# Second attention of a two-layer kernel: blocks from last to first, the causal mask subtracted by VectorE, products a step later

## The reference, cut to what matters

```python
def _forgetting_attention(q, k, v, log_f):
    scale = ATT_HEAD_DIM ** -0.5
    fcum = jnp.cumsum(log_f, axis=-1)
    for blk in range(seqlen // ATT_BLOCK):          # 8 blocks of 128 queries
        q0, q1 = blk * ATT_BLOCK, (blk + 1) * ATT_BLOCK
        s = jnp.einsum('bhqd,bhkd->bhqk', q[:, :, q0:q1], k[:, :, :q1]) * scale
        s = s + fcum[:, :, q0:q1, None] - fcum[:, :, None, :q1]
        s = jnp.where(kpos[None, :] <= qpos[:, None], s, -jnp.inf)
        prob = jax.nn.softmax(s, axis=-1)
        outs.append(jnp.einsum('bhqk,bhkd->bhqd', prob, v[:, :, :q1]))
```

## Time and profile before

| | |
|---|---|
| time, median of 3 runs | 2603.03 us (2601.33 to 2605.16) |
| the profiled execution: its time, its span | 2604.71 us, 2602.9 us |
| TensorE busy, share of the span | 2530.3 us, 97% |
| VectorE, ScalarE, GpSimd busy | 1580.3, 1225.1, 1134.3 us |
| granted TensorE clock, mean | 0.991 |
| second attention | from about 1838 to 2330 us |

### The profile page before, as it was taken

The page is one execution under the profiler, slowest core; times in us unless marked ns, Lnnn a source line. Parts: engine busy times, 40 slices in busy tenths (PEclk is TensorE's granted clock), DMA queues, the critical chain, the costliest instruction groups (busy, mean ns, idle before and its releaser), DMA issues.

```text
span 2602.9 us, 32821 instructions
## 1 busy us (share of the span) xinstructions
PE 2530.3 (97%) x12946; PEld 2120.4 (81%) x12946; DVE 1580.3 (61%) x2413; ACT 1225.1 (47%) x1858; POOL 1134.3 (44%) x759
## 2 busy tenths in 40 slices
PE   5999999999999999999999999999999999999998
PEld 3788898877888888878788888888888888888886
DVE  7554899487555556665833367665666666654333
ACT  4243888344444443342543435543666666642132
POOL 0222444439787863444487234333322222235233
PEclk8999999999999999999999999999999999999998
DMA  6133001322222226553232322222111111167452
GB/s 272 65 121 130 1 1 66 114 79 92 89 81 78 92 102 242 179 174 122 90 117 102 122 73 90 90 84 71 65 49 49 49 59 60 54 213 273 148 184 97
DMA packets 84457, 275.81 MB, mean 106 GB/s; under 512 B 9392, under 2 KB 9520, under 8 KB 84304
## 3 DMA queue, kind: packets, MB, share of 16 engines
q1 hardware_dynamic: 84304, 273.71, 30.0%
HBM read 219.54 MB, written 54.13 MB: 105 GB/s over the span
## 4 chain that ended last, share of the span: by engine, by line
PE 81%; DVE 9%; ACT 5%; DMA 2%; issue 1%; POOL 1%; SPq 0%; DVEq 0%; ACTq 0%; POOLq 0%
PE ps L614 12%; PE ps L616 12%; PE ps L615 12%; PE ps L991 7%; PE ps L992 7%; PE ps L993 7%; PE ps L857 5%; PE ps L834 4%; PE ps L810 2%; PE ps L811 2%; PE ps L1048 2%; DVE wf L3056 2%; PE ps L1049 2%; PE ps L1050 2%; DVE wf L3081 1%
## 5 line engine op out<-in xcount | busy, mean ns | idle before, releaser
L3383 POOL TENSOR_TENSOR hl<-raw,hl 128x1024 fp32r<-128x1024 f32 x161 | 403.9, 2511 | 933.9 <-ACT hl L1407 933.5
L614 PE MATMUL ps<-ht,hl 128*128 128x512 f32 x1552 | 633.4, 408 | 15.0 <-DVE ht L2456 9.9
L616 PE MATMUL ps<-ht,hl 128*128 128x512 f32 x1552 | 608.3, 392 | 0.0
L615 PE MATMUL ps<-ht,hl 128*128 128x512 f32 x1552 | 607.8, 392 | 0.0
L614 PEld LDWEIGHTS ps<-ht,hl 128*128 128x128 f32 x1552 | 293.5, 189 | 75.4 <-DVE ht L2456 9.9
L616 PEld LDWEIGHTS ps<-ht,hl 128*128 128x128 f32 x1552 | 292.8, 189 | 64.1
L615 PEld LDWEIGHTS ps<-ht,hl 128*128 128x128 f32 x1552 | 294.0, 189 | 53.8 <-issue 1.5
L3459 POOL TENSOR_SCALAR wf<-wf,st 128x1024 f32<-128x1024 f32 (+2 forms) x192 | 168.8, 879 | 318.7 <-DVE st L2589 318.7
L1407 ACT ACTIVATE hl<-raw 128x1024 fp32r<-128x1024 f32 x163 | 171.3, 1053 | 178.9 <-PE ps L1050 66.6
L2396 DVE TENSOR_TENSOR ps<-ps,wf 128x512 f32<-128x512 f32 x116 | 80.8, 697 | 152.3 <-PE ps L993 152.1
L834 PE MATMUL ps<-cst,wf 128*128 128x128 f32 x1088 | 151.4, 274 | 3.8 <-POOL wf L3459 3.8
(11 more groups left out here) (287 smaller groups left out, 5314.8 us busy)
## 6 DMA issues: line engine op xcount, KB each, us to landing
raw<-in_wst SPq DMA_DIRECT2D x243, 512.0 KB, 3.6
wf<-scratch_rows SPq DMA_DIRECT2D x32, 512.0 KB, 5.0
scratch_g<-wf SPq DMA_DIRECT2D x22, 512.0 KB, 2.6
wf<-scratch_g SPq DMA_DIRECT2D x44, 256.0 KB, 4.2
wf<-in_xT SPq DMA_DIRECT2D x16, 512.0 KB, 7.7
htf<-in_wst SPq DMA_DIRECT2D x16, 512.0 KB, 15.4
scratch_ys<-wr SPq DMA_DIRECT2D x16, 512.0 KB, 4.5
ht<-scratch_ys SPq DMA_DIRECT2D x32, 256.0 KB, 5.9
```

The costliest lines, as they stand in the source:

```text
L614: self.op.matmul(out, wh, xh[:, c], start=(j == 0), stop=False)
L615: self.op.matmul(out, wh, xl[:, c], start=False, stop=False)
L616: t = self.op.matmul(out, wl, xh[:, c], start=False, stop=(j == kt - 1))
L3383: self.op.tensor_tensor(K.hl[:, u * 2048 + 1024:u * 2048 + 2048], K.raw[:, i % 3 * 1024:(i % 3 + 1) * 1024], hi.bitcast(F32), ALU.subtract ...
```

## The change

It has five parts, all in the second attention.

1. Every head's query blocks go from 7 to 0: a block in step `s` has `8 - s % 8` key blocks where it had `s % 8 + 1`. A pair of blocks for `back` now begins with the longer one, so `back` takes its length from the odd block number.
2. The mask matmul L815 is gone. VectorE has a new method `mask`: one subtraction of 128 x 128 from the forget-gate row in SBUF, once for each block, ahead of the `top` that reads it.
3. `back` for a pair stands at odd steps, right behind the scores and ahead of the fillers, on blocks `s - 3` and `s - 2`; it stood at even steps behind the transposes, on blocks `s - 2` and `s - 1`. ScalarE and VectorE copy its product out ahead of their part of `turn`.
4. On VectorE the reciprocal `soft(s + 1)` stands behind `top(s + 2)` and `mask(s + 3)`, where it was `soft(s + 2)` at the end of step `s`; the transposes' low part is last in the step. ScalarE's and GpSimd's orders stay, but for the place of `back`.
5. `fills` has another table. The number of fillers in a pair stays: 24 in steps -2 to 13 (27 for the last pair).

```diff
@@ fills
-    if s < 2:
-        return (0, 3 if p == 7 else 2, 3, 3)[s + 2]
     if p == 7 and s > LAST_FILL:
         return {13: 1, 14: 4, 16: 3}.get(s, 0) if own else 0
     if p == 7:
-        return (2, 1, 2, 1, 2, 2, 2, 1, 2, 1, 2)[s - 2]
-    return 2 if s in (4, 6, 10, 12) else int(s < 14)
+        return (0, 3, 4, 1, 3, 1, 3, 1, 2, 1, 3, 1, 2, 1, 1)[s + 2]
+    return (0, 3, 4, 1, 3, 1, 2, 0, 2, 0, 3, 1, 2, 0, 2, 0)[s + 2] if s < 14 else 0
@@ TensorEngine.scores
-            t = self.op.matmul(out, qs, K.wrr(kl)[:, c], start=False, stop=not diag)
-            if diag:
-                self.consts()
-                self.wait_ge(*K.at("maskr"))
-                t = self.op.matmul(K.ps[pair][:, nk - 128:nk], K.idr[:, :], K.maskr[:, :],
-                                   start=False, stop=True)
+            t = self.op.matmul(out, qs, K.wrr(kl)[:, c], start=False, stop=True)
@@ TensorEngine.back
-        nk = qt + 1 if causal else 8
+        nk = (qt | 1) + 1 if causal else 8
...
-            c0 = 128 if causal and j == qt else 0
+            c0 = 128 if causal and j == nk - 1 else 0
@@ TensorEngine.attend2
                 if s + 2 < 16:
                     sc(s + 2)
+                if s >= 3 and s % 2 == 1:
+                    g = 16 * p + s - 2
+                    hi, lo, _ = pt2(K, (g // 2) % 2)
+                    self.back(2, g, 7 - (s - 2) % 8, hi, lo, 6 + (s - 2) // 8, True,
+                              (("vstack2", p),))
                 self.fill(fills(p, s, True))
...
                 if 0 <= s < 16:
-                    self.turn(2, 16 * p + s, s % 8, 9 + (16 * p + s) % 3, True)
-                if s >= 2 and s % 2 == 0:
-                    g = 16 * p + s - 1
-                    hi, lo, _ = pt2(K, (g // 2) % 2)
-                    self.back(2, g, (s - 1) % 8, hi, lo, 6 + (s - 1) // 8, True,
-                              (("vstack2", p),))
+                    self.turn(2, 16 * p + s, 7 - s % 8, 9 + (16 * p + s) % 3, True)
@@ VectorEngine
+    def mask(self, h, qt):
+
+        K = self.K
+        c = K.w(20 + h % 2)[:, qt * 128:qt * 128 + 128]
+        self.wait_ge(*K.at("fcum", h))
+        self.wait_ge(*K.at("maskr"))
+        self.op.tensor_tensor(c, c, K.maskr[:, :].bitcast(F32),
+                              ALU.subtract).then_inc(*self.done("masked", h, qt))
@@ VectorEngine.attend2
                 if s + 2 < 16:
-                    self.top(2, g + 2, 2 * p + (s + 2) // 8, (s + 2) % 8, 9 + (g + 2) % 3, True)
+                    if s == -2:
+                        self.mask(2 * p, 7)
+                    self.top(2, g + 2, 2 * p + (s + 2) // 8, 7 - (s + 2) % 8, 9 + (g + 2) % 3, True)
+                    if s + 3 < 16:
+                        self.mask(2 * p + (s + 3) // 8, 7 - (s + 3) % 8)
...
+                if 0 <= s + 1 < 16:
+                    self.soft(2, g + 1)
+                if s >= 3 and s % 2 == 1:
+                    self.back(2, g - 2, (s - 2) // 8, 7 - (s - 2) % 8, w(22))
                 if 0 <= s < 16:
-                    self.turn(2, g, s % 8, pt2(K, (g // 2) % 2), True)
-                if s + 2 < 16:
-                    self.soft(2, g + 2)
-                if s >= 2 and s % 2 == 0:
-                    self.back(2, g - 1, (s - 1) // 8, (s - 1) % 8, w(22))
+                    self.turn(2, g, 7 - s % 8, pt2(K, (g // 2) % 2), True)
```

More of the change, by code:

```diff
@@ L805, in scores @@
             out = K.ps[pair][:, c]
-            diag = causal and c.stop == nk
             self.bank_free(2 * pair + half)
@@ L841, in back @@
         K = self.K
-        nk = qt + 1 if causal else 8
+        nk = (qt | 1) + 1 if causal else 8
         for gg in (g - 1, g):
-            for half in range((((qt if gg == g else qt - 1) + 1 if causal else 8) + 3) // 4):
+            for half in range(((qt + g - gg + 1 if causal else 8) + 3) // 4):
                 self.wait_ge(*K.at("plo", A, gg, half))
@@ L1286, in sc @@
                 k = 2 + 2 * h
-                self.scores(2, 16 * p + s, 2 * p + h, s % 8, h, k, k + 1, True,
+                self.scores(2, 16 * p + s, 2 * p + h, 7 - s % 8, h, k, k + 1, True,
                             (("stacklo", "q2", p, h), ("stacklo", "k", p, h),
@@ L2206, in attend2 @@
                 g = 16 * p + s
+                if s >= 3 and s % 2 == 1:
+                    if s == 3 and p:
+                        self.wait_ge(*K.at("stored_ya", p - 1))
+                    self.back(2, g - 2, (s - 2) // 8, 7 - (s - 2) % 8, w(22))
                 self.fill(fills(p, s))
@@ L2213, in attend2 @@
                 if 0 <= s < 16:
-                    self.turn(2, g, s % 8, pt2(K, (g // 2) % 2)[0], True)
+                    self.turn(2, g, 7 - s % 8, pt2(K, (g // 2) % 2)[0], True)
                 if s + 2 < 16:
-                    self.soft(2, g + 2, (s + 2) % 8, 9 + (g + 2) % 3, True)
-                if s >= 2 and s % 2 == 0:
-                    if s == 2 and p:
-                        self.wait_ge(*K.at("stored_ya", p - 1))
-                    self.back(2, g - 1, (s - 1) // 8, (s - 1) % 8, w(22))
+                    self.soft(2, g + 2, 7 - (s + 2) % 8, 9 + (g + 2) % 3, True)
                 if s == 15 and p < 7:
@@ L2575, in top @@
             if g >= 3:
-                self.wait_ge(*K.at("turn", A, g - 3, ((g - 3) % 8) // 4))
-            self.wait_ge(*K.at("fcum", h))
+                self.wait_ge(*K.at("turn", A, g - 3, (7 - (g - 3) % 8) // 4))
+            self.wait_ge(*K.at("masked", h, qt))
             self.op.tensor_tensor_reduce(pw, ps, K.w(20 + h % 2)[:, 0:nk], 1.0, -3.0e38,
@@ L3674, in attend2 @@
                 if s + 2 < 16:
-                    self.weigh(2, g + 2, (s + 2) % 8, 9 + (g + 2) % 3, True)
+                    self.weigh(2, g + 2, 7 - (s + 2) % 8, 9 + (g + 2) % 3, True)
                 if p == 7 and s == LAST_FILL:
```

## The result

The changed kernel takes 2626.94 us in the median (2624.21 to 2628.03), beside 2604.1 us for the kernel before, measured with it: a ratio of 1.0087, with a 95% interval of 1.0075 to 1.0100. It is 23 us slower, where 2587 us and at most 2597 were forecast. The profiled execution has a span of 2626.2 us.

The account below looks back on a forecast made before the run. The prediction took TensorE's queue of matmuls, busy 59.79 of 60 us, as the bound. Its terms -13.3 - 2.9 + 0.5 = -15.7 us took 2604.71 to 2589.0, a median of 2587 us expected, range 2582 to 2597.

Parts of the forecast that it names:

- The step on new waits: Budget of TensorE's work against the other engines' chain in each of a pair's 16 steps; claimed +0.5 us in all.
- The mask's price: 128 mask matmuls taken off TensorE at 0.11 us each, less 0.8 us kept by followers: -13.3 us (-14.1 to -10.9).
- The first distance alone: Rival: only the 0.06 us from mask to next start is the mask's price, 7.7 us, total 2593 us; chance 0.12.
- The 10.4 us: Alternative estimate for the 128 masks from the skill's 81 ns spacing of 128-column matmuls; whole change then 12.8 us.
- The follower's 0.05 us behind short scores: TensorE matmuls behind scores ending in a short part may keep 0.05 us without the mask; bounds 0 to 3.2, taken 0.8.
- The wait of `back`: TensorE's products no longer wait for the transposes' low part, in 7 of 8 pairs: 7 x 0.41 = -2.9 us.
- The distances between the other matmuls: Scores, transposes, products and fillers on TensorE keep number and width, only neighbours change: 0, with +-1 us.
- The other side's rival: VectorE's mask, with two SBUF operands, is shut out while GpSimd works, mostly on `weigh`: 2613 us, slower by 0.4%; chance 0.08.
- The slack: At the narrowest block, 3 key blocks (steps 5 and 13): TensorE's 3.9 us against the chain's 3.5, leaving 0.4 us.
- The +0.5 us for step 1: Step 1's transposes may wait for step 0's low part to free their bank: 0 to 0.1 us, 8 times, taken +0.5.

Follow-up runs that it names:

- experiment 3: Kernel before, with only VectorE's copy of a pair's last product moved behind the low parts of the next keys; 2646.73 us, ratio 1.0166.
- experiment 1: Changed kernel with VectorE's copy of a pair's last product (L2613) again ahead of the next keys' low parts; 2593.13 us, ratio 0.9953 to the kernel before.
- experiment 2: Changed kernel with SyncE loading the next pair's forget-gate rows ahead of the wait for the pair's product and its store; 2591.79 us, ratio 0.9948 to the kernel before.
- experiment 4: experiment 1 with the mask matmul back on TensorE and no subtraction on VectorE; 2600.85 us, ratio 0.9987 to the kernel before.
- experiment 6: experiment 1 and experiment 2 together, plus a pair's first mask issued in step 17 of the pair before; 2585.99 us, ratio 0.9935 to the kernel before.
- experiment 5: Kernel before, old block order, with only the mask moved to VectorE and no L815 (result not the reference's); 2620.3 us, ratio 1.0063.
- experiment 8: experiment 6 with each mask subtraction on VectorE done twice, 128 more instructions; 2595.66 us, 9.7 us above experiment 6.
- experiment 10: experiment 6 with one filler of the last pair moved from step 14 to step 15; 2590.59 us, ratio 0.9944 to the kernel before.

## Why the prediction was wrong

**What failed.** The step on new waits. It worked out the budget of each of the 16 steps from one block's transposes to the next but one, inside a pair. The border between two pairs was in none of them, and the whole term for new waits was +0.5 us. On VectorE the change carries L2613 of the last two blocks past `late`, the low parts of the next keys, with the wait in front of them. The prediction listed `back`'s new place but followed only TensorE's, where its position at the border is the same as before. On SyncE, the store and the loads of the next rows are queued behind this copy, which the earlier trace rows cannot show, since before it cost TensorE nothing. Shown by experiment 3 (+42 us by this move alone), by experiments 1 and 2 (-34 and -35 us against the changed kernel by two different cures), and by the trace: the third scores wait 26.7 us, of which 3.4 remain in experiment 1. Compared matmul by matmul with experiment 1, the seven waits are 23.3 us longer and the matmuls behind them, mostly at the lower clock, 13.3: 36.6 of the 36.8 us between the two stages. No term of the prediction has the lower clock behind a wait.

**The mask's price was right.** -13.3 us were forecast. The stages of experiments 4 and 6 differ by 14.0 us (486.1 - 472.1), which is 0.109 us a mask, and their times by 14.9 (14.3, each against the kernel before beside it). The first distance alone (0.06 x 128 = 7.7) is refuted. The 10.4 us, by the spacing of 81 ns that the Trainium skill gives on the page "TensorE: Matmul & The Clock Gate" (back-to-back issue gap), is short of the measurement too. The follower's 0.05 us behind short scores: in experiment 1 a filler behind scores of 256 columns takes 0.23 to the next start, behind 128 columns 0.29. So it stays behind 128 columns only, for 8 fillers (0.06 each) and, by 12 products in 1.42 us, about 0.03 for 24 groups of products: 1.2 us, where I had taken 0.8.

**The wait of `back` was right, its agreement with the total was luck.** -2.9 us were forecast, and experiment 4 has -2.7 in the stage and -3.2 in the time. The wait is gone there, as forecast. But to the end of its last products the stage is 4.1 us shorter, and that is made of three parts. The wait is 2.9. The distances between the other matmuls are 4.1 less, which the prediction had at 0 with +-1. And three new waits in the last pair take 2.9 back, with 1.6 us more behind the stage. The prediction has none of these waits.

**The other side's rival named a real mechanism at the wrong place.** The shut-out by GpSimd came true: 1.70 us at the first mask of each pair but the first, with 3.4 us of waits in experiment 1. It is not in the prediction, since it looked for splits between steps -2 and 13 and found only that of step 2. The first one, fetched with the fillers ahead of step -2, meets the pair's first mask. (In the changed kernel that mask takes 0.29 us, since the late rows hold it back until the split is over.) But `weigh` does not meet the masks in the new order: the median of L2583 is its 0.28 us, its mean 0.32, and its 8 long rows all stand behind splits. In the old order the same rival comes true in full (experiment 5). What the Trainium skill states on the page "SBUF — State Buffer", section "SBUF: two separate sides", that VectorE with two SBUF operands and GpSimd lock each other out for a whole instruction, agrees with these rows: the blocked masks end within 0.15 us of GpSimd's instruction (1898.91 and 1898.76, 1850.56 and 1850.42).

**The slack** of 0.4 us held where I worked it out: with every mask done twice the transposes of 3 key blocks come without a wait. It was too large for step 4 (experiment 8). The +0.5 us for step 1 does not show: in experiment 6 the transposes of that step follow their filler after the usual 0.23 us and take their usual time.

With the copy in order, the rows early and the first mask out of GpSimd's way, the forecast of 2587 us is met by 2585.99, in part by luck, since the smaller distances and the waits of the last pair, neither of them forecast, nearly cancel. That is also the time of another kernel; for the one that was to be predicted, 2587 was wrong by 40 us.

## What to carry to other kernels

When an instruction is moved past others, write down for each engine, SyncE's queue included, who is queued behind it, and follow that at the borders of a loop as well as inside, where the next iteration's loads hang on the last iteration's stores. A saturated engine hides how little slack the queues beside it have: here a load 7 us late made waits of 3.5 to 4.7 us, and about half of each was lost again at the lower clock. An instruction of VectorE with two operands in SBUF should be put where GpSimd is idle, and its price read from its longest row, not only from its median. A block at the border of a loop, or in its last turn, needs a budget of its own.

## What was not expected of the hardware

After an idle time of 3.3 to 4.0 us TensorE soon had some 5 to 13 matmuls 0.43 us apart instead of 0.23 (1905.82, 1906.25, 1906.67 above), the lower of its two clock levels, 1.2 GHz. It returned to 0.23 without a further break. In 7 pairs of the changed kernel the matmuls behind the waits took some 13 us more, beside 26.7 of waiting. In experiment 1, where the idle times of the stage are 0.4 to 1.6 us, no such stretch is seen. In between it went both ways: 6 to 8 such matmuls stood behind idle times of 1.88 and 1.90 us in experiment 8 and of 1.99 in experiment 10, and none behind 1.87 in experiment 2.
